# The sub-norm of a differential-attention head: squares summed as two fp32r parts, one projection later

## The reference, cut to what matters

```python
def rms_norm(x, w):
    xf = x.astype(jnp.float32)
    y = xf * lax.rsqrt(jnp.mean(xf * xf, axis=-1, keepdims=True) + EPS)
    return (y * w.astype(jnp.float32)).astype(x.dtype)
...
        a = diff_attention(dq, dk, dv, lam, DIFF_HEAD_DIM ** -0.5)
        a = rms_norm(a, diff_subln_w[i]) * (1.0 - lam_init)
        y_a = a.reshape(b, s, DIFF_V_WIDTH) @ w_o_diff[i]
```

## Time and profile before

| | |
|---|---|
| median of 3 executions | 2023.81 us (2023.42 to 2023.92) |
| the profiled execution | 2023.66 us |
| its span, first to last instruction | 2021.8 us |
| PE busy | 1988.0 us, 98% of the span |
| DVE, ACT, POOL busy | 51%, 44%, 54% |
| mean granted TensorE clock | 0.997 |
| DMA | 213 MB, mean 105 GB/s |

### The profile page before, as it was taken

How to read it: one execution, slowest core, us unless ns; L and a number is a source line. 1 busy time by engine, 2 the same in 40 slices (tenths; PEclk the granted TensorE clock), 3 DMA queues, 4 the chain that set the end, 5 groups by cost and what they waited for, 6 DMA issues and landing times.

```text
span 2021.8 us, 29003 instructions
## 1 busy us (share of the span) xinstructions
PE 1988.0 (98%) x9357; PEld 1635.9 (81%) x9357; DVE 1023.1 (51%) x1767; ACT 884.6 (44%) x1548; POOL 1083.4 (54%) x1424
## 2 busy tenths in 40 slices
PE   6999999999999999999999999999999999999997
PEld 5888788888888888888888788878878888888886
DVE  6445777776754433321134657777766543333211
ACT  6434555555634332233344445555564432322332
POOL 6556344444465555557764644444436555555673
PEclk9999999999999999999999999999999999999999
DMA  6333223223553333333353332322245423333232
GB/s 219 104 112 105 73 75 88 84 68 94 193 161 99 94 96 101 93 113 92 99 167 92 101 94 83 83 69 83 82 133 187 133 87 102 96 102 91 86 93 84
DMA packets 358545, 213.01 MB, mean 105 GB/s; under 512 B 15478, under 2 KB 343228, under 8 KB 357692
## 3 DMA queue, kind: packets, MB, share of 16 engines
q1 hardware_dynamic: 342462, 173.87, 30.1%
q10 hardware_dynamic: 15998, 38.04, 5.3%
HBM read 191.40 MB, written 20.45 MB: 105 GB/s over the span
## 4 chain that ended last, share of the span: by engine, by line
issue 40%; POOL 38%; PE 20%; POOLq 1%; ACT 0%; DMA 0%; DVE 0%; SPq 0%; ACTq 0%; DVEq 0%
POOL w_lo L549 38%; PE proj L587 7%; PE proj L588 7%; PE proj L589 7%; POOLq L554 0%; POOLq L552 0%; DMA raw<-in_w_out 0%; PE flip L969 0%; ACT y_out L1468 0%; POOL rope_t L540 0%; PE score L988 0%; PE score L599 0%; POOL freq L523 0%; POOLq L549 0%; DVE x_sum L1627 0%
## 5 line engine op out<-in xcount | busy, mean ns | idle before, releaser
L549 POOL TENSOR_TENSOR w_lo<-raw,w_hi 128x256 fp32r<-128x256 f32 x1376 | 1077.7, 815 | 914.8 <-ACT w_hi L1006 913.8
L587 PE MATMUL proj<-h_hi,w_hi 128*128 128x512 f32 (+1 forms) x1616 | 645.2, 399 | 0.0
L589 PE MATMUL proj<-h_hi,w_lo 128*128 128x512 f32 (+1 forms) x1616 | 630.6, 390 | 0.0
L588 PE MATMUL proj<-h_lo,w_hi 128*128 128x512 f32 (+1 forms) x1616 | 629.9, 390 | 0.0
L1006 ACT ACTIVATE w_hi<-raw 128x1024 fp32r<-128x1024 f32 x344 | 362.8, 1056 | 207.0 <-DMA raw<-in_w_down 58.5
L587 PEld LDWEIGHTS proj<-h_hi,w_hi 128*128 128x128 f32 (+1 forms) x1616 | 303.6, 188 | 64.7 <-issue 4.4
L588 PEld LDWEIGHTS proj<-h_lo,w_hi 128*128 128x128 f32 (+1 forms) x1616 | 303.6, 188 | 64.6 <-issue 3.8
L589 PEld LDWEIGHTS proj<-h_hi,w_lo 128*128 128x128 f32 (+1 forms) x1616 | 303.2, 188 | 64.8
L587 PE MATMUL proj<-hid_hi,w_hi 128*128 128x512 f32 x352 | 137.6, 391 | 0.0
L589 PE MATMUL proj<-hid_hi,w_lo 128*128 128x512 f32 x352 | 137.1, 389 | 0.0
L588 PE MATMUL proj<-hid_lo,w_hi 128*128 128x512 f32 x352 | 137.0, 389 | 0.0
(11 more groups left out here) (384 smaller groups left out, 3015.0 us busy)
## 6 DMA issues: line engine op xcount, KB each, us to landing
raw<-in_w_in SPq DMA_DIRECT2D x232, 256.0 KB, 3.1
raw<-in_w_gate_up SPq DMA_DIRECT2D x176, 256.0 KB, 3.0
raw<-in_w_down SPq DMA_DIRECT2D x96, 192.0 KB, 2.5
gate_in<-gate_scratch ACTq DMA_DIRECT2D x48, 256.0 KB, 3.4
gate_scratch<-gate_out ACTq DMA_DIRECT2D x46, 256.0 KB, 2.0
raw<-in_w_mem_kv SPq DMA_DIRECT2D x32, 256.0 KB, 2.9
raw<-in_w_o_diff SPq DMA_DIRECT2D x32, 256.0 KB, 3.0
raw<-in_w_out SPq DMA_DIRECT2D x32, 256.0 KB, 2.9
```

Of the source, the lines that this page charges most:

```text
L549: ins = g.tensor_tensor(w_lo[s][:, cols], raw[s % 2][:, cols], w_hi[s][:, cols].bitcast(F32), ALU.subtract)
L587: mm(o, hi[:, c:c + width], rh, start=start and k == 0, stop=False)
L588: mm(o, hi[:, c:c + width], rl, start=False, stop=False)
L589: ins = mm(o, lo[:, c:c + width], rh, start=False, stop=stop and k == n - 1)
```

## The change

For heads 0 to 6 of each layer (14 in all; head 7 keeps the old way):

- ScalarE squares `att` twice, once to fp32 (`a_sq`) and once to fp32r (`sq_hi`); VectorE subtracts the two into an fp32r remainder (`sq_lo`) in a new function, `square_low`, at the end of the iteration.
- TensorE no longer issues the squares' fp32 matmul at the end of the iteration. It issues two fp32r matmuls (`head_squares`) with a new fp32r matrix of ones in the next iteration, behind unit 0.
- ScalarE's `rms` and VectorE's `out_diff` of head h-1 move into iteration h: `rms` behind the exponentials of the latent scores and the first `split_ahead`, `out_diff` behind the maxima of the first differential map.
- GpSimd fills `ones_r` once at the start. `sq_hi` and `sq_lo` lie in memory that is unused at that time or shared with `att_low`.

```diff
+        ones_r = here("ones_r", [P, P], F32R)
...
+        sq_hi = at("sq_hi", 46 * KB, [P, SEQ], F32R)
+        sq_lo = at("sq_lo", T + 38 * KB, [P, SEQ], F32R)
...
+            def head_squares(l, h):
+
+                pe.wait_ge(a_split.sem, a_split.at(l, "B", h, 1))
+                mm(proj[1][:, :], ones_r[:, :], sq_hi[:, :], start=True, stop=False)
+                mm(proj[1][:, :], ones_r[:, :], sq_lo[:, :], start=False, stop=True).then_inc(ssq_full.sem, 1)
+
...
                      KD, h_rhs, w=w(0)).then_inc(slot_done.sem, 1)
+                if h:
+                    pe.wait_ge(diff_ready.sem, diff_ready.at(l, "B", h, 2))
+                    head_squares(l, h - 1)
                 pe.wait_ge(qk_split.sem, qk_split.at(l, "B", h, 2))
...
                 flip_values(l, n)
 
-                pe.wait_ge(a_squared.sem, a_squared.at(l, "B", h, 1))
-                pe.wait_ge(diff_ready.sem, diff_ready.at(l, "B", n, 2))
-                mm(proj[1][:, :], ones[:, :], a_sq[:, :], start=True, stop=True).then_inc(ssq_full.sem, 1)
...
                 sc.activation(a_sq[:, :], att[:, :], ACT.Square, scale=float(P) ** -0.5).then_inc(a_squared.sem, 1)
+                if h < HEADS - 1:
+                    sc.activation(sq_hi[:, :], att[:, :], ACT.Square, scale=float(P) ** -0.5).then_inc(a_squared.sem, 1)
...
                 split_ahead(l, "B", h, 0, h)
+                if h:
+                    rms(l, "B", h - 1, 0, proj[1])
                 query_rows(l, n)
...
                 values_high(l, n)
-                act.wait_ge(att_read.sem, att_read.at(l, "B", h))
-                rms(l, "B", h, 0, proj[1])
...
+            def square_low(l, h):
+
+                ve.wait_ge(a_squared.sem, a_squared.at(l, "B", h, 2))
+                ve.wait_ge(att_read.sem, att_read.at(l, "B", h, 1))
+                v.tensor_tensor(sq_lo[:, :], a_sq[:, :], sq_hi[:, :].bitcast(F32), ALU.subtract).then_inc(a_split.sem, 1)
+
...
                 maxima(l, "B", h, 1, "d1", DIFF_SCALE)
+                if h:
+                    out_diff(l, h - 1)
                 causal_low(l, h, 0, 0)
...
                 values_low(l, n)
-                out_diff(l, h)
+                square_low(l, h)
```

More of the change, by code:

```diff
@@ L304, in build_trunk @@
         ckv_squared = Tally(sem("ckv_squared"), "act", A=(2, 1))
-        a_squared = Tally(sem("a_squared"), "act", B=(1, HEADS))
+        a_squared = Tally(sem("a_squared"), "act", B=(2, HEADS - 1), L=(1, 1))
+        a_split = Tally(sem("a_split"), "ve", B=(1, HEADS - 1))
         NORM = dict(A=(QT + KVT, 1), F=(4, 2), H=(2, 4))
@@ L349, in build_trunk @@
             *gate_loaded, gate_scaled, ssq_full, ssq_read, rms_ready, tile_ready, ckv_copied,
-            ckv_squared, a_squared, pair_ready, pair_hi, pair_lo, gl_ready, memh_hi, memh_lo,
+            ckv_squared, a_squared, a_split, pair_ready, pair_hi, pair_lo, gl_ready, memh_hi, memh_lo,
             outs_split_hi, outs_split, sig_ready, od_used, om_used, oc_used, mix_ready,
@@ L529, in _ @@
             g.memset(ones[:, :], 1.0)
+            g.memset(ones_r[:, :].bitcast(F32), 1.0)
             g.memset(eps[:, :], EPS)
@@ L749, in last_head @@
                 causal_attend(l, h)
-                pe.wait_ge(a_squared.sem, a_squared.at(l, "B", h, 1))
+                pe.wait_ge(a_squared.sem, a_squared.at(l, "L", 0, 1))
                 pe.wait_ge(gate_copied.sem, gate_copied.at(l, "L", 0, 4))
```

## The result

| | before | after |
|---|---|---|
| median, first measurement | 2023.62 us (4 executions, 2022.97 to 2023.92) | 2010.89 us (4, 2010.40 to 2012.57) |
| median, second measurement, on another occasion | 2023.27 us (9) | 2010.69 us (5, 2010.42 to 2011.13) |
| span of the profiled execution | 2021.8 us | 2009.3 us |

The ratio of after to before is 0.9939, 95% interval 0.9926 to 0.9952: 12.7 us less, where 12.9 had been forecast. The second measurement gives 0.9936 (0.9922 to 0.9949).

A forecast was written before the change was run, and what follows sets the result against it. TensorE, busy 98% of the span, was taken to bound the kernel. 14 x (1.38 removed - 0.46 added) = 12.9 us off 2023.66 gives 2010.8, or 2010.9 us as median; range 2009.5 to 2014.5.

The forecast's parts named there:

- TensorE sets the time in the heads: Head loop: TensorE, busy 98% of the span, sets the time; a microsecond taken out of its stream comes off the end.
- What is removed, 1.38 us a head: Iteration's end, value transposes to unit 0's second matmul: 2.05 us becomes 0.67, 19.3 us over 14 heads.
- Its two parts: Before unit 0: 0.40 us waiting for ScalarE's square, 0.97 us for the fp32 matmul and the switch back.
- What is added, 0.46 us a head: Two fp32r matmuls on TensorE between unit 0 and the scores, at 0.228 us each; 6.4 us, up to 12.7.
- The inputs and the Ln: `sq_lo` ready at about 247.8, 2.7 us early; moved Ln ends at 251.95, 1.3 us before unit 1; cost 0.
- the prediction's d: At unit 1, which must wait for the Ln: if the Ln were late by d, each head would lose d.
- called tight: ScalarE's `pt_hi`: Exp and query copy end at about 253.2, TensorE's transposes come at 253.22; no delay expected.
- Cost 0: VectorE's 1.44 us of new work falls into idle time or before the rotated queries, 2.36 us early; none reaches TensorE.
- A: Between unit 0 and the scores the pair brings gaps of 0.1 to 0.46 us; 2012.3 to 2017.4 us; 12 in 100.
- B: Ahead of unit 1 the Ln replaces the square as TensorE's wait; losing 0.92 us a head gives 2023.8; 5 in 100.
- C: Squares' pair: fp32r matmuls no faster than fp32, 0.97 us each, 7.8 us slower, 2031.6 us; 2 in 100.
- D: Earlier exponentials loosen other TensorE seams, at most 1 or 2 us more gain, to 2009; 3 in 100.

The follow-up runs named there:

- the place alone: Against the kernel before: one plain fp32 squares matmul moved behind unit 0 with the scaling, no second square or remainder; 2016.93 us, ratio 0.9965.
- The two runs with a late Ln: Changed kernel with 2 or 4 needless ScalarE copies between the sum's arrival and the Ln, heads 0 to 6; 2011.94 and 2031.12 us.
- the split alone: Against the kernel before: two fp32r squares matmuls at the old place before unit 0, scaling at its old place; 2034.96 us, ratio 1.0055.

## Why the prediction was right

**TensorE sets the time in the heads.** Shown from both sides: two paces more a head gave 6.4 us more, one pace less gave 2.8 less, while 2.2 us more on VectorE gave nothing and 1.2 us more on ScalarE gave 1 us, with an iteration that was no longer than the changed kernel's.

**What is removed, 1.38 us a head.** Right as a sum: 2.05 us became 0.69, which is 1.36. Its two parts were mis-sized, by 0.10 us each. The fp32 matmul itself costs 0.87 us, and 0.10 of the "0.97 us" that the prediction put down to the matmul "and the switch back" is the pick-up behind the wait, which the place removes and not the split. By the Trainium skill ("FP8 and Floating Point Precision", TensorE Precision Notes) a true fp32 matmul makes four passes, by the estimate 0.91 us; the 0.87 of the kernel with the place alone agrees with the rule better than the 0.97 that the sum was made with. The sum did not suffer, because both parts go.

**What is added, 0.46 us a head.** Right: 0.45 in the rows, and 6.4 us for a second pair. The two further waits in TensorE's program cost nothing, having been met 2.8 us before (`sq_lo` through at 247.68, the pair at 250.53).

**The inputs and the Ln.** `sq_lo` was forecast for 247.8, the Ln's end for 251.95 and its margin at 1.3 us; they are 247.68, 251.87 and 1.4. The two runs with a late Ln bracket the margin. Beyond it a head lost a little more than the prediction's d: 1.36 us for the 1.1 by which the Ln was too late. ScalarE's `pt_hi`, called tight, has 0.16 us of idle time left and did not slip.

**VectorE.** Cost 0, and the run with 2.2 us more on it agrees. The prediction named the rotated queries, 2.36 us early, as the next thing that TensorE wants of VectorE. That was not quite it: the transposes that reuse a bank behind the first subtraction come sooner in TensorE's order, and they, not the queries, stalled in the run with 4.3 us more.

**The rivals.** A, gaps in the pair, is excluded by the pair issued twice and by the rows from unit 0 to the scores. B, the Ln as the new wait, does not happen, and does from a delay between 1.2 and 2.5 us on. C, fp32r squares at the price of fp32, is excluded by the same rows as A. Its sentence that splitting gains only if each matmul is a quarter of the old price was wrong, and disagrees with the 0.69 us that it goes on to give: two matmuls gain as soon as each is under half of what they replace. D did not show. What the prediction did not say is that the two halves of the change are unlike: the place alone wins 6.8 us, the split alone loses 11.3, and together they win 12.7.

## What to carry to other kernels

On an engine that is always busy, a reduction at the end of an iteration costs its own time and the wait for its input; moved behind the next independent block of work, it gives the wait back at once, and a preparation that the new place hides, such as splitting an operand in two for cheaper matmuls, becomes free, as long as the other engines have the slack. Here that slack was 1.4 us for the Ln. Judge such a preparation only together with the place: here the same split was worth -11 us at the old place and +6 at the new one. And before a further bit is taken off, see who is next in line: half a microsecond saved at the last head came back as a wait 11 us later.

## What the runs showed of the hardware

**VectorE beside GpSimd.** Two small copies on VectorE took 0.84 and 0.86 us in the changed kernel, and 0.42 us each in the run with six needless multiplications, where they came later. In the first case GpSimd was splitting weights at the time, in the second it had finished (258.12 + 3.40 = 261.52, the copy at 262.43). The first iteration of a layer has no multiplications, and in the first layer's the two copies still took 0.84 and 0.87 us beside GpSimd in that same run. The rows of the changed kernel, from its timeline of all engines:

```profile
256.47 1.80 DVE L1556 TENSOR_SCALAR p_b<-p_b,inv_d 128x128 f32<-128x128 f32 x4
...
257.25 3.37 POOL L554 TENSOR_TENSOR w_lo<-raw,w_hi 128x256 fp32r<-128x256 f32 x4 [4.68 <-ACT w_hi L1018]
...
258.30 0.84 DVE L1598 COPY mqT<-gate_in 32x512 f32<-32x512 f32 x1
```

That gave back 0.87 us of the 4.3. But a delay does not always shrink in this way. In the run with three multiplications the copies took 0.42 us as well, while the scaling of the probabilities ahead of them (`p_b`) had moved beside GpSimd's work and took 2.93 us instead of 1.80, so more was lost than gained:

```profile
256.92 2.99 POOL L555 TENSOR_TENSOR w_lo<-raw,w_hi 128x256 fp32r<-128x256 f32 x4 [4.68 <-ACT w_hi L1019]
...
257.26 2.93 DVE L1557 TENSOR_SCALAR p_b<-p_b,inv_d 128x128 f32<-128x128 f32 x4
...
260.23 0.42 DVE L1599 COPY mqT<-gate_in 32x512 f32<-32x512 f32 x1
```

The expectation for that run had the rotated queries 1.35 us later. They were 1.4 us later (through at 266.06, where everything lies 0.33 us earlier than in the changed kernel), but partly by luck, since it counted neither effect. Not everything slows: the subtraction behind the copies (`pt_lo`, 128x384), which reads one operand from PSUM, took 0.54 us beside GpSimd and 0.54 without it. The Trainium skill ("GPSIMD Engine Reference", Specifications) says that GpSimd's interfaces to the local memory are shared with VectorE, with contention for VectorE instructions in a 2-port performance mode or with two inputs in that memory. These rows agree in that some VectorE instructions slow down beside GpSimd and others do not; whether the slowed ones ran in that mode no row shows. No run here varied GpSimd's work alone, so the cause is argued from the overlap, not shown.

**Picking up behind a wait.** An fp32r matmul that picks up behind a wait is dearer than one in a stream: the pair at the old place took 0.54 us to unit 0's first slot, in the stream 0.45. Most of the difference lies between its first two starts, 246.02 and 246.32, which are 0.30 us apart where the stream has 0.23.
